# The decay levels of a gated recurrent mixer: six levels instead of eight, the last one a product over blocks of four

## What is computed

```python
f = lb + (1.0 - lb) * sigmoid(f_lin); k = 1.0 - f; q = silu(q_lin)
b = cumsum(log f)                      # within a chunk
scores[t, s] = sum_k q[t, k] * exp(b[t, k] - b[s, k]) * k[s, k]    # s <= t
o = scores @ v + (q * exp(b)) @ state
```

## Time and profile before

| | |
|---|---|
| median of 3 runs | 1674.55 us (1673.82 to 1676.05) |
| span of the profiled execution | 1672.5 us |
| its own device time | not listed apart from the runs; they lie 1.3 to 3.6 us above the span |
| TensorE busy | 1623.2 us, 97% |
| VectorE busy | 1083.9 us, 65% |
| ScalarE, GpSimd busy | 694.1 and 660.1 us |
| mixer with its dense jobs | 118.16 to 341.37 us |
| value jobs of the attention | 341.37 to 384.6 us |

### The profile page before, as it was taken

One profiled execution on the slowest core, in us unless ns is written; L12 is line 12 of the kernel. 1 busy time (PEld: TensorE's weight loads), 2 busy tenths in 40 slices (PEclk: granted clock), 3 DMA queues, 4 the chain that ended last, 5 costly groups with the idle time before them and its releaser, 6 DMA issues.

```text
span 1672.5 us, 21299 instructions
## 1 busy us (share of the span) xinstructions
PE 1623.2 (97%) x8016; PEld 1356.4 (81%) x8016; DVE 1083.9 (65%) x1682; ACT 694.1 (41%) x1083; POOL 660.1 (39%) x468
## 2 busy tenths in 40 slices
PE   5999999999999999999999989999999999999996
PEld 4888888888888878878887878888888888888886
DVE  7649888635777610035606679987666679857977
ACT  3244454236888740021133553454454453333342
POOL 2132122331332243333445298666655513332334
PEclk9999999999999999999999999999999999999999
DMA  8111101111001121111334525455433498868672
GB/s 286 70 51 39 26 26 27 38 39 39 26 26 52 39 76 51 44 45 51 101 89 127 190 98 176 170 204 177 155 139 140 167 345 272 265 187 235 198 218 101
DMA packets 204854, 200.79 MB, mean 120 GB/s; under 512 B 8521, under 2 KB 174665, under 8 KB 202705
## 3 DMA queue, kind: packets, MB, share of 16 engines
q1 hardware_dynamic: 201584, 188.35, 35.9%
q10 hardware_dynamic: 3168, 11.08, 1.7%
HBM read 153.23 MB, written 46.17 MB: 119 GB/s over the span
## 4 chain that ended last, share of the span: by engine, by line
PE 84%; DVE 6%; ACT 4%; issue 2%; POOL 2%; DMA 2%; SPq 1%; ACTq 0%; DVEq 0%; POOLq 0%
PE dense L877 12%; PE dense L867 7%; PE dense L869 7%; PE dense L871 6%; PE dense L1180 4%; PE dense L1182 3%; PE dense L1181 3%; PE dense L1260 3%; PE dense L1262 3%; PE dense L1261 3%; PE mixA L1002 3%; PE mixA L1180 2%; PE mixA L1181 2%; PE mixB L1181 2%; PE mixA L1182 2%
## 5 line engine op out<-in xcount | busy, mean ns | idle before, releaser
L877 PE MATMUL dense<-parts 128*128 128x512 f32 x1008 | 246.6, 396 | 1.3 <-ACT page L1343 1.3
L757 POOL CAST parts<-page 128x1024 fp32r<-128x1024 f32 x55 | 60.6, 1103 | 450.6 <-PE dense L871 208.4
L877 PEld LDWEIGHTS dense<-parts 128*128 128x128 f32 x1008 | 184.3, 188 | 36.9 <-POOL parts L760 1.5
L760 POOL TENSOR_TENSOR parts<-page,parts 128x512 fp32r<-128x512 f32 x134 | 191.1, 1447 | 46.1 <-ACT parts L1594 41.7
L867 PE MATMUL dense<-parts 128*128 128x512 f32 x544 | 191.2, 413 | 1.7 <-DVE parts L2097 1.2
L869 PE MATMUL dense<-parts 128*128 128x512 f32 x544 | 179.5, 392 | 0.0
L871 PE MATMUL dense<-parts 128*128 128x512 f32 x544 | 178.7, 390 | 0.0
L841 POOL TENSOR_TENSOR parts<-page,parts 128x512 fp32r<-128x512 f32 x52 | 87.1, 1696 | 208.8 <-ACT parts L1715 208.8
L803 POOL TENSOR_TENSOR page<-page 128x512 f32<-128x512 f32 x80 | 121.7, 1521 | 65.6 <-PE dense L1182 25.7
L811 POOL TENSOR_TENSOR parts<-page,parts 128x512 fp32r<-128x512 f32 x80 | 114.7, 1436 | 50.7 <-ACT parts L1641 44.4
L871 PEld LDWEIGHTS dense<-parts 128*128 128x128 f32 x544 | 102.3, 188 | 22.7
(11 more groups left out here) (247 smaller groups left out, 3894.4 us busy)
## 6 DMA issues: line engine op xcount, KB each, us to landing
page<-in_w_ff SPq DMA_DIRECT2D x104, 512.0 KB, 5.8
page<-act_scratch SPq DMA_DIRECT2D x56, 512.0 KB, 5.6
page<-in_w_in SPq DMA_DIRECT2D x90, 256.0 KB, 3.3
act_scratch<-page SPq DMA_DIRECT2D x16, 1024.0 KB, 3.9
act_scratch<-page SPq DMA_DIRECT2D x16, 768.0 KB, 7.0
page<-in_w_o SPq DMA_DIRECT2D x32, 256.0 KB, 3.1
h_scratch<-page ACTq DMA_DIRECT2D x8, 512.0 KB, 2.8
page<-c_scratch SPq DMA_DIRECT2D x8, 512.0 KB, 5.2
```

Source lines behind the costliest of these rows:

```text
L760: ins = nc.gpsimd.tensor_tensor(R(lo, at, HALF), F(raw_page(c), at, HALF), R(hi, at, HALF).bitcast(F32), ALU.subtract)
L877: ins = mm(o, wlo if n == 2 else whi, x_, start=first and n == 0, stop=last and n == 2)
```

## The change

LEVELS goes from 8 to 6. Levels 0 to 4 (m = 64 to 4) stay. The levels with m = 2 and m = 1 and the diagonal are replaced by one product over blocks of four tokens: q is scaled by exp(b - mid) and k by exp(mid - b), where mid is the mean of b at the second and third token of the block, both in place, and the mask takes s <= t within the block. Its exponentials (two for each half) go to PG_AB and PG_T2; the sums of the middles are made once per head in a new tile `mids`. A head has 20 steps on TensorE instead of 24; so that the stream has its 24 groups, four steps (3, 6, 9 and 12) have two. The forget columns' low parts are put into columns 64 to 71 of their own high tile, so that two products (the tile by hi, the tile by lo) give all four combinations; the low rows come out in partitions 64 to 71, from where ScalarE copies them and VectorE adds them. This product lo by lo was not there before.

```diff
-LEVELS = 8
+LEVELS = 6
+HL = 2 * LEVELS
+LOW_AT = 64
-BESIDE = {4: (46, 47), 5: (48, 49), 19: (33, 40), 24: (42, 43),
+BESIDE = {4: (46, 47), 5: (48, 49), 19: (33, 33), 24: (42, 43),
+HG_TWICE = (3, 6, 9, 12)
...
+                if c == 19:
+                    rows8 = lambda v, at: v.rearrange("q (k n) -> q k n", k=KD)[:, :, at:at + NFX]
+                    nc.gpsimd.tensor_tensor(rows8(R(hi), LOW_AT), rows8(F(raw_page(c)), 0), rows8(R(hi), 0).bitcast(F32),
+                                            ALU.subtract).then_inc(w_split, 1)
+                    continue
...
+                if hi == lo:
+                    for k in range(KD):
+                        xs = halves(acts_hi[k]) + halves(acts_lo[k])
+                        for n, (o, x_) in enumerate(zip(2 * halves(dense[SET[j]][:, :]), xs)):
+                            ins = mm(o, R(hi, k * P, P), x_, start=k == 0 and n < 2, stop=k == KD - 1 and n >= 2)
...
-            for step in range(HG_LEAD + 24 * NHG):
+            for _ in range(HG_LEAD):
                 next(stream)
-                if step >= HG_LEAD:
-                    hg_step(*divmod(step - HG_LEAD, 24))
+            for step in range((HL + 8) * NHG):
+                n, i = divmod(step, HL + 8)
+                for _ in range(2 if i in HG_TWICE else 1):
+                    next(stream)
+                hg_step(n, i)
...
             def level_exp(n, hl):
-                act.wait_ge(ab_sub, 14 * n + hl + 1)
+                act.wait_ge(ab_sub, HL * n + hl + 1)
                 ab = F(PG_AB + (hl % 4) // 2, (hl % 2) * HALF, HALF)
+                if hl >= HL - 2:
+                    A(F(PG_T2, (hl % 2) * HALF, HALF), ab, ACT.Exp, scale=-1.0)
                 A(ab, ab, ACT.Exp).then_inc(ab_exp, 1)
...
             for k in range(3):
                 head_high(0, k)
             tmp = F(PG_XP)[0:NFX, :]
+            done(act, "crow")
+            nc.scalar.copy(tmp, out_of("crow")[LOW_AT:LOW_AT + NFX, :]).then_inc(c_low, 1)
...
+                if hl >= HL - 2:
+                    fours = lambda v: v.rearrange("q (a n) -> q a n", n=4)
+                    twice_mid = mids[:, hf * P:(hf + 1) * P].rearrange("q (a n) -> q a n", n=1).to_broadcast([P, P, 4])
+                    dve.wait_ge(qe_ready, n + 1)
+                    V.scalar_tensor_tensor(out=fours(F(PG_AB + (hl % 4) // 2, (hl % 2) * HALF, HALF)), in0=twice_mid,
+                                           scalar=-0.5, in1=fours(F(PG_HB + n % 2, hf * HALF, HALF)),
+                                           op0=ALU.mult, op1=ALU.add).then_inc(ab_sub, 1)
+                    return
...
+                if hl >= HL - 2:
+                    q, k = F(PG_HQ + n % 2, hf * HALF, HALF), F(PG_HK + n % 2, hf * HALF, HALF)
+                    dve.wait_ge(ab_exp, HL * n + hl + 1)
+                    V.tensor_tensor(k, k, F(PG_T2, hf * HALF, HALF), ALU.mult)
+                    V.tensor_tensor(q, q, F(PG_AB + (hl % 4) // 2, (hl % 2) * HALF, HALF), ALU.mult).then_inc(ab_ready, 1)
+                    return
...
-                for i in range(19):
+                for i in range(HL + 3):
...
+                    if i == 4:
+                        b = F(PG_HB + n % 2).rearrange("q (a n) -> q a n", n=4)
+                        V.tensor_tensor(mids.rearrange("q (a n) -> q a n", n=1), b[:, :, 1:2], b[:, :, 2:3], ALU.add)
...
-                        if i == 15:
+                        if i == HL:
                             f_part(n + 1)
-                        if i == 17:
+                        if i == HL + 1:
                             decay_part(n + 1)
...
             done(dve, "crow")
-            V.tensor_scalar(z, out_of("crow")[0:NFX, :], fb[0:NFX, :], None, ALU.add).then_inc(c_lin, 1)
+            dve.wait_ge(c_low, AFTER_LB + 1)
+            V.scalar_tensor_tensor(out=z, in0=out_of("crow")[0:NFX, :], scalar=fb[0:NFX, :], in1=tmp,
+                                   op0=ALU.add, op1=ALU.add).then_inc(c_lin, 1)
...
-    masks[:, LEVELS - 1, :] = s == t
+    masks[:, LEVELS - 1, :] = (s // 4 == t // 4) & (s <= t)
```

More of the change, by code:

```diff
@@ L371, in block_kernel @@
         k_hi = sem("k_hi")
+        c_low, AFTER_LB = lb_exp, 1
         heads_high = lambda hh: NHG + (3 * hh + 3 if hh < 2 else hh + 5)
@@ L898, in feature_job @@
                 hi, lo = PARTS[CHUNK_OF[j]]
+                if hi == lo:
[3 more added lines that the diff above has]
+                            ins = mm(o, R(hi, k * P, P), x_, start=k == 0 and n < 2, stop=k == KD - 1 and n >= 2)
+                        if k == KD - 1:
+                            end(ins, j)
+                        yield
+                    return
                 xs = cut(acts_hi[0])
@@ L1007, in hg_step @@
                     ins.then_inc(lvl_done, 1)
-                elif i < 20:
-                    u = i - 18
-                    pe.wait_ge(pred_done, 16 * n + 14 + u + 1)
+                elif i < 4 + HL:
+                    u = i - 2 - HL
+                    pe.wait_ge(pred_done, HL * n + HL - 2 + u + 1)
                     pe.wait_ge(kt_done, 2 * n + u + 1)
@@ L1016, in hg_step @@
                     ins.then_inc(upd_done, 1)
-                elif i < 22:
-                    hf = i - 20
+                elif i < 6 + HL:
+                    hf = i - 4 - HL
                     pe.wait_ge(st_ready, 2 * n + hf + 1)
                     pe.wait_ge(qe_ready, n + 1)
-                    pe.wait_ge(pred_done, 16 * n + 16)
+                    pe.wait_ge(pred_done, HL * n + HL)
                     for c in range(4 * hf, 4 * hf + 4):
@@ L1402, in _ @@
                 q_page, b_page = PG_HQ + nxt % 2, PG_HB + nxt % 2
-                for hl in range(14):
+                for hl in range(HL):
                     if n == 0 or hl >= 2:
@@ L1421, in _ @@
                         sig_end(q_page, q_exp)
-                    elif hl == 11:
+                    elif hl == 8:
                         if n:
@@ L1425, in _ @@
                         sig_exp(b_page, "f", nxt)
-                    elif hl == 12:
+                    elif hl == 9:
                         sig_log(b_page)
-                    elif hl == 13:
+                    elif hl == 10:
                         sig_end(b_page, f_exp)
@@ L1876, in _ @@
             for c in range(4):
-                V.tensor_copy(masks[:, 0:LEVELS - 1, 64 * c:64 * c + 64], F(PG_T2).rearrange("q (a n) -> q a n", n=P)[:, 0:LEVELS - 1, 0:64])
+                V.tensor_copy(masks[:, 0:LEVELS - 1, 64 * c:64 * c + 64], F(PG_T2, 0, LEVELS * P).rearrange("q (a n) -> q a n", n=P)[:, 0:LEVELS - 1, 0:64])
                 ins = V.tensor_copy(masks[:, LEVELS - 1, c * P:(c + 1) * P], F(PG_T2, (LEVELS - 1) * P, P))
@@ L1989, in _ @@
             for n in range(NHG):
-                for i in range(19):
-                    if i < 14 and (n == 0 or i >= 2):
+                for i in range(HL + 3):
+                    if i < HL and (n == 0 or i >= 2):
                         level_sub(n, i)
-                    if 1 <= i < 15 and (n == 0 or i >= 3):
+                    if 1 <= i < HL + 1 and (n == 0 or i >= 3):
                         level_mul(n, i - 1)
```

23 lines of the change are left out of this document (11 added, 12 removed).

## The result

The changed kernel takes 1659.14 us (median of 4 runs, 1658.01 to 1660.29) against 1674.18 for the kernel before (median of 4): a ratio of 0.9907, with a 95% interval of 0.9896 to 0.9919. The forecast was 1660.7, in a range of 1656 to 1665; the profiled span was forecast at 1658.6 and is 1658.5. The changed kernel ran twice more, among the experiments: 1659.70 and 1660.34, ratios 0.9909 and 0.9915.

The account below looks back on a forecast made before the run. TensorE, busy 97%, was taken as the bound; -14.6 - 1.8 - 1.8 + 1.8 + 0.9 + 1.6 = -13.9 us takes the span from 1672.5 to 1658.6, and 2.05 us to the median gives 1660.7 us, range 1656 to 1665.

Parts of the forecast that it names:

- The removed half levels: Mixer on TensorE: 16 half levels a head become 12, at 0.91 us each over four heads, 14.6 us less.
- What VectorE pays: Mixer heads: VectorE loses about 10 us busy and gains 5.0 a head, hidden under TensorE, so nothing put.
- Waits that go: Heads 0 and 3: TensorE's three waits for the take of a level all vanish, 1.8 us less.
- Waits that come: Heads 0 to 2: TensorE waits four times for VectorE's gate or query multiplication, 0.45 us each, 1.8 us more.
- Forget job inside head 3: Four shorter forget groups before and between head 3's last steps bring the last averaging product 1.8 us earlier.
- The longer chain: Forget sums ahead of the third value job: ScalarE's copy makes them later, 18.5 us against 17.6, 0.9 us more.
- The clock: Behind TensorE's stall of about 3.1 us before the third value job, half speed costs 1.6 us more.
- The rest, let move rigidly: Behind the value jobs, loads, splits and casts follow TensorE's progress, so no change in time was put there.
- a sign of being wrong: Behind the value jobs: idle time differing by more than 2 us from before would show the prediction wrong.
- half of the gain given back: Rival, 8%: POOL and DMA waits behind 384.6 grow; with half the gain given back, 1667 us.
- The tail of a head: End of each head: VectorE's last take done at 212.1, TensorE asks at 212.7, so 0.6 us spare.
- two falls of the clock behind waits: Before 28.43 and 899.03, waits of 3.06 and 2.04 us preceded clock 0.50; rival, clock stays up, 20%, 1659.1 us.

Follow-up runs that it names:

- doubles_and_forget: Changed kernel with double groups in steps 4, 6, 10 and 12 and VectorE's forget part in step 11, not 12; 1657.08 us (one run).
- split_first: Changed kernel with VectorE's split of the first value job ahead of the scan of the forget sums, not behind it; 1657.53 us, ratio to before 0.9902.
- levels_only: Changed kernel with the forget columns as before (three products, 48 matmuls, no copy by ScalarE); 1661.59 us, ratio to before 0.9920.
- copy_earlier: Changed kernel with ScalarE's copy of the low forget rows behind the first of three casts, not the third; 1658.75 us, ratio to before 0.9912.
- doubles_later: Changed kernel with the double groups in steps 4, 6, 10 and 12, not 3, 6, 9 and 12; 1660.04 us, ratio to before 0.9914.
- filled_wait: Changed kernel with 12 more matmuls, results unread, ahead of the third value job; 1660.00 us, ratio to before 0.9913.
- all_three: Changed kernel with the first value split ahead of the scan, doubles in steps 4, 6, 10, 12, forget part in step 11; 1653.71 us, ratio to before 0.9879.

## Why the prediction was right

Point by point, in D and from start to start:

- *The removed half levels*: -14.6 forecast. A head without any wait takes 51.34 us (doubles_and_forget) against 55.07: 3.73 for four, so -14.9.
- *What VectorE pays*: the subtraction with the four-fold repeated middle was taken at 0.75 us, with 1.5 as its upper bound; it takes 0.68 (head 1, 189.72), and the products on 512 columns 0.68 too. No wait for them is listed. What met GpSimd's splits were two products on 256 columns, at 1.46 and 1.51 us.
- *Waits that go*: -1.8 forecast, and -2.45 measured: the three listed waits had moved the products at 125.61, 289.11 and 292.62 by 0.61, 0.49 and 1.23 from start to start, and the steps behind them took another 0.1. I had taken the listed idle time. The causes were those named: the double group for head 0, the double group and the small split for head 3, where either does most of it alone.
- *Waits that come*: four, in the places forecast, each 0.3 listed; +1.8 forecast, 2.35 measured by the lengths of the heads, 0.59 for each wait and not 0.45.
- *Forget job inside head 3*: -1.8, measured 1.84.
- *The longer chain*: +0.9; from the last averaging product to the third value job there are 18.43 us where there were 17.60, so +0.83, with 18.5 forecast. VectorE's addition took 1.27, not 1.37. The 17.2 from which the forecast took TensorE's arrival at 15.4 has no row (17.60 less the listed 0.22 is 17.4), but in split_first, which has no wait there, TensorE arrives at 15.5.
- *The clock*: +1.6; between the third value job and the scores 34.09 us against 32.73, so +1.36; in five other profiles with a fall there it is 1.6.
- *The rest, let move rigidly*: 0 forecast, +0.46 measured, and not rigidly. The wait of 2.04 us before 899.03, behind which the clock fell (one of the two places from which its price was taken), is 1.11 us after the change, and the granted clock stays at 1.00. From the first scores to the next product that waits behind that place (927.78, now 911.86) the changed kernel is therefore 1.4 us faster. In the last stage it gives this back at the wait for the split, 1.68 us where there were 0.32. TensorE's idle time behind the first scores grew by 1.9 us, from 28.2 to 30.1, just short of the 2 us that the prediction had named as a sign of being wrong.

The window of TensorE behind that wait of 1.11 us in the changed kernel:

```profile
884.00:885.00 1.00, 1.00 (x11) 1.00 0.94 330
```

The measured terms of D, -14.9 - 2.45 + 2.35 - 1.84 + 0.83 + 1.36, make -14.65; D moved by -14.6 and the forecast sum was -13.9. The misses of 0.65 and 0.55 us on the waits cancel. That the span came out within 0.1 us of 1658.6 is luck in part: D moved by 0.7 us more than forecast, and the start and the rest, for which nothing was put, by 0.6 the other way. One rival has a slip of no weight: half of the gain given back makes 1667.6, not 1667.

Two steps of the argument were off without moving the forecast. The tail of a head was said to have 0.6 us to spare. It has next to none. ScalarE's logarithm waits for VectorE's forget part, and the scan for the logarithm; the scan now stands one step behind the forget part in VectorE's list and not two. These are the two in head 1 of the changed kernel:

```profile
200.59 1.06 ACT L1382 ACTIVATE page<-page 128x1024 f32<-128x1024 f32 x1 [4.10 <-DVE page L1927]
...
201.68 2.63 DVE L1934 TENSOR_TENSOR_SCAN page<-ones,page 128x128 f32<-128x128 f32 x8 [0.23 <-ACT page L1382]
```

The scan waits for the logarithm; before, the logarithm was done at 206.16 and the scan began at 207.54, behind a take. And two falls of the clock behind waits were taken as a rule, with 20% against it. Of the eight profiles with a long wait of the third value job seven have the fall, and that of doubles_and_forget has not.

The change is made of a part that pays (the levels) and a part that pays nothing on top: levels_only and the whole change have the same D. By the terms above, the forget columns' part brings 1.84 us in head 3 and, with the double group in place, 0.5 by GpSimd's shorter split; the longer chain takes 0.83 of this back, and the clock 1.36. The other half of its products, 1.8 us behind the last averaging product, is off the queue of the bounding engine, but that engine then waits for the chain all the same.

## What to carry to other kernels

When the bounding engine is 97% busy, count the work that leaves its queue by start-to-start distances, then walk its queue and ask for each buffer who frees it and what stands ahead of that in the other engine's list: both the four waits of 0.3 us and the one of 2.9 were to be read from the trace before. A wait costs more than its listed time, 0.6 for 0.3 here, and where the clock fell behind a wait of 2 to 3 us it cost 1.4 to 1.6 more. What lies behind the change need not move rigidly: here a slow stretch went and a wait grew, and only the near cancelling of the two, 1.4 us each, kept the rest where it was. Moving the head of a late chain (0.4 us) was worth less than taking the consumer's own piece out of it (4.3 us).

## What the runs showed of the hardware

The clock does not fall behind every long wait. TensorE stood 2.89 us in the changed kernel, 2.27 in copy_earlier and 2.87 in doubles_later, and the granted clock was 0.50 for some 3 us behind each; it stood 2.87 us at the same place in doubles_and_forget and the clock stayed at 1.00. The other long waits agree: at the one before 899.03 (in the kernel before) the clock fell behind 2.04 us there and 2.18 in levels_only, but not behind 2.10 in filled_wait; at the one in the last stage it fell behind 1.98 us in split_first, but not behind 2.24 in all_three. The work around each place is the same, so the length of the wait alone does not decide it. What does, no run here tells. The price when it falls is 1.4 to 1.6 us, less when the slow stretch begins while TensorE still stands. These are the windows of TensorE in doubles_later, where it comes back at 336.45 and the fall comes a us later:

```profile
336.00:337.00 1.00, 0.55 (x3) 1.00 0.23 33
337.00:338.00 1.00, 1.00 (x5) 0.72 0.00 0
```

Two VectorE operations took longer beside GpSimd than I had counted on. The scan of 1024 elements in eight partitions took 2.27 or 2.28 us alone (twelve profiles) and 3.33 while one of GpSimd's subtractions on 64 partitions ran. The sum of the middles, 256 columns, took 0.60 us in head 0 and 1.74 in heads 1 and 2 of the changed kernel:

```profile
125.51 0.60 DVE L2039 TENSOR_TENSOR mids<-page 128x256 f32<-128x256 f32 x1
...
175.84 1.74 DVE L2039 TENSOR_TENSOR mids<-page 128x256 f32<-128x256 f32 x1
...
174.58 2.52 POOL L771 TENSOR_TENSOR parts<-page,parts 128x512 fp32r<-128x512 f32 x2
```

GpSimd's two subtractions run from 174.58 to 177.10; the sum starts within them, at 175.84, and ends at 177.58, 0.5 us behind them. In all_three, where the double group comes later, this sum starts before them, at 173.40 and 224.75, and takes 0.61 and 0.60 us.
